# Attention of one core: VectorE combines a unit between the next one's two minima, ScalarE copies transposed probabilities between two exponentials

## The reference, cut to what matters

```python
# 4 heads, 1024 tokens, causal; q and k have two components of 64 each, v has 128
a[c] = softmax(q[:, c] @ k[:, c].T + causal_mask)          # c = 0, 1
attn = rms_norm((a[0] - lam * a[1]) @ v) * subln_w * (1 - lambda_init)
# recurrence, per group of 128 channels (4 groups)
r, i = sigmoid(xc @ w_gate_a + b_a), sigmoid(xc @ w_gate_x + b_x)   # xc: 4-tap causal conv
h[t] = exp(-8 * softplus(lru) * r) * h[t-1] + sqrt(1 - decay**2) * i * xc
y = h * gelu(gr)
```

## Time and profile before

| | us |
|---|---|
| median of 3 runs | 4649.63 (4648.69 to 4650.72) |
| profiled execution | 4649.02 |
| its span | 4647.2 |
| TensorE busy | 4526.9 (97% of the span) |
| VectorE busy | 2670.9 (57%) |
| ScalarE busy | 1728.5 (37%) |
| attention stage | about 3547 to 3743 of the span |

### The profile page before, as it was taken

How to read it: one execution, slowest core, us unless ns; L and a number is a source line. 1 busy time by engine, 2 the same in 40 slices (tenths; PEclk the granted TensorE clock), 3 DMA queues, 4 the chain that set the end, 5 groups by cost and what they waited for, 6 DMA issues and landing times. The chain is left out here.

```text
span 4647.2 us, 66517 instructions
## 1 busy us (share of the span) xinstructions
PE 4526.9 (97%) x27608; PEld 3674.0 (79%) x27608; DVE 2670.9 (57%) x3938; ACT 1728.5 (37%) x2924; POOL 457.6 (10%) x371
## 2 busy tenths in 40 slices
PE   7999999999999999999999799899999989999999
PEld 4888877778999999999999444688777567888887
DVE  3245545555637777777777686546453755555543
ACT  3234443444424544555444333211343742111111
POOL 0000000000002333332335000000010000000000
PEclk8999999999999999999999999999999999999999
DMA  5244344434430110111021352423210021122222
GB/s 210 99 145 150 131 147 141 145 132 150 168 120 15 46 54 33 62 43 59 28 100 47 98 179 86 150 104 118 82 46 19 19 113 64 68 77 73 100 87 95
DMA packets 155978, 441.79 MB, mean 95 GB/s; under 512 B 17168, under 2 KB 47120, under 8 KB 140448
## 3 DMA queue, kind: packets, MB, share of 16 engines
q1 hardware_dynamic: 140624, 383.98, 23.8%
q0 software_dynamic: 9296, 32.58, 2.0%
q10 hardware_dynamic: 5760, 20.97, 1.2%
HBM read 294.86 MB, written 141.56 MB: 94 GB/s over the span
## 5 line engine op out<-in xcount | busy, mean ns | idle before, releaser
L202 PE MATMUL pr_ps<-uhl,w_split 128*128 128x512 f32 (+1 forms) x1520 | 586.1, 386 | 3.1 <-DVE w_split L145 2.2
L206 PE MATMUL pr_ps<-uhl,w_split 128*128 128x512 f32 (+1 forms) x1520 | 571.1, 376 | 0.0
L205 PE MATMUL pr_ps<-uhl,w_split 128*128 128x512 f32 (+1 forms) x1520 | 570.6, 375 | 0.0
L1583 DVE TENSOR_TENSOR b_G<-b_ps,cst 128x512 fp32r<-128x512 f32 x560 | 381.4, 686 | 65.1 <-PE b_ps L1362 61.7
L138 ACT ACTIVATE w_split<-share 128x2048 fp32r<-128x2048 f32 x64 | 122.6, 1915 | 700.8 <-DVE ou_vc L3304 271.1
L202 PEld LDWEIGHTS pr_ps<-uhl,w_split 128*128 128x128 f32 x1520 | 286.7, 189 | 81.5 <-issue 29.2
L205 PEld LDWEIGHTS pr_ps<-uhl,w_split 128*128 128x128 f32 x1520 | 286.9, 189 | 56.1 <-issue 5.8
L206 PEld LDWEIGHTS pr_ps<-uhl,w_split 128*128 128x128 f32 x1520 | 286.6, 189 | 52.6
L1124 POOL TENSOR_SCALAR b_Mr<-b_tri 128x512 fp32r<-128x512 f32 x80 | 117.7, 1489 | 1878.4 <-DVE b_tri L1567 1878.4
L202 PE MATMUL ou_ps<-ou_a,w_split 128*128 128x512 f32 x704 | 277.1, 394 | 7.7 <-DVE ou_a L2160 7.7
L205 PE MATMUL ou_ps<-ou_a,w_split 128*128 128x512 f32 x704 | 275.4, 391 | 0.0
(11 more groups left out here) (498 smaller groups left out, 10082.3 us busy)
## 6 DMA issues: line engine op xcount, KB each, us to landing
w_ring<-in_w_in SPq DMA_DIRECT2D x41, 1024.0 KB, 5.5
proj<-pr_stage SPq DMA_DIRECT2D x160, 256.0 KB, 2.0
share<-in_w_up SPq DMA_DIRECT2D x24, 1024.0 KB, 4.8
ar<-share SPq DMA_DIRECT2D x32, 512.0 KB, 2.8
b_AR<-ar SPq DMA_DIRECT2D x64, 256.0 KB, 2.9
pr_raw<-proj SPq DMA_DIRECT2D x48, 256.5 KB, 3.5
ada<-in_ada_w SPq DMA_DIRECT2D x24, 512.0 KB, 5.6
ff<-ou_vc ACTq DMA_DIRECT2D x24, 512.0 KB, 2.6
```

The source lines that it names most:

```text
L202: mm = nc.tensor.matmul(dst, a[0], b[0], start=start, stop=False)
L205: nc.tensor.matmul(dst, a[0], b[1], start=False, stop=False)
L206: return nc.tensor.matmul(dst, a[1], b[0], start=False, stop=stop)
L1583: L[x]["dve"].done(V.tensor_tensor(Gs[x][m % 2][:], heads(x, 0 if m else 1), rep(K(f"lev{m}"), 4), ALU.mult), f"{n}.G{m}")
```

## The change

TensorE's `sc` takes one component: its order becomes sc(n, 0), tr(n-2), sc(n, 1), then gates or flip, then av(n-3), one unit later than before. ScalarE: exp(n, 0), turn_out(n-2), take(n-3), exp(n, 1), then the work of t. VectorE: peak(n, 0), soft(n-1), peak(n, 1), then the work of t. The sums are kept for a whole head (`sm` grows to two heads of eight units), so that the reciprocal of component 0 is taken once per head in `mean`, `soft` takes that of component 1 alone and its copy to `r0` goes. Work moves between units: square from 1 to 3, mean from 2 to 4, norm from 4 to 5, scale from 5 to 6, run from 7 to 0 of the next head (head 3's stays at 7), leave from 0 to 1, the taps from 4 to 7 to 1 to 4. ScalarE gets two explicit loads of function tables, the set with Ln and Exp behind `rise`, and that with Exp and Tanh ahead of `open_a` in heads 1 to 3; the Ln on a dummy before the end goes.

```diff
--- before.py
+++ after.py
@@ -2587,7 +2587,7 @@
         sem = lambda m: nc.alloc_semaphore(f"at_{m}")
         sb = lambda n, s, d=F32: ctx.enter_context(nc.sbuf_tensor("at_" + n, s, d))
         p, aT = sb("p", [P, 2, 2, T]), sb("aT", [P, 2, T // P, P])
-        nb, sm, rc = sb("nb", [P, 2, 2]), sb("sm", [P, 2, 2]), sb("rc", [P, 2, 2])
+        nb, sm, rc = sb("nb", [P, 2, 2]), sb("sm", [P, 2, 8, 2]), sb("rc", [P, 2])
         ratio = sb("ratio", [P, 2])
         r0 = sb("r0", [P, 2, 8])
         lp, lam = sb("lp", [P, 2]), sb("lam", [P, 4])
@@ -2615,7 +2615,6 @@
         y_stored, head_stored = ([sem(f"{n}{b}") for b in range(2)] for n in ("y_stored", "stored"))
         S = ps[:, 0:4].rearrange("p (c b) f -> p c (b f)", c=2)
         TR = ps[:, 4:6].rearrange("p a f -> p (a f)")
-        warm = ctx.enter_context(nc.sbuf_tensor("at_warm", [P, 1], F32))
         flat_at = lambda h, x: ps[:, 4 + x] if h + 1 == A_HEADS else ps[:, 1 + 2 * x]
         with nc.Block() as block:
             @block.sync
@@ -2643,19 +2642,18 @@
                 nc.tensor.matmul(ps[:, 7, 0:2], K("heads64"), lp[:], start=True, stop=True).then_inc(lam_s, 1)
                 pe.wait_ge(rounded, 2)
 
-                def sc(n):
+                def sc(n, c):
                     h, t = units[n]
                     w = (t + 1) * P
-                    if t == 4:
+                    if t == 4 and c == 0:
                         pe.wait_ge(th_x, h + 1)
-                    for c in range(2):
-                        if n >= 1:
-                            pe.wait_ge(exp_ready, 2 * n - 1 + c)
-                        r = slice(64 * c, 64 * c + 64)
-                        for b in range(0, w, HALF):
-                            nc.tensor.matmul(S[:, c, b:min(w, b + HALF)], qk[r, h, t * P:(t + 1) * P],
-                                             qk[r, 4 + h, b:min(w, b + HALF)], start=True, stop=b + HALF < w)
-                        nc.tensor.matmul(S[:, c, t * P:w], id_r[:], mask_r[:], start=False, stop=True).then_inc(scores, 1)
+                    if n >= 1:
+                        pe.wait_ge(exp_ready, 2 * n - 1 + c)
+                    r = slice(64 * c, 64 * c + 64)
+                    for b in range(0, w, HALF):
+                        nc.tensor.matmul(S[:, c, b:min(w, b + HALF)], qk[r, h, t * P:(t + 1) * P],
+                                         qk[r, 4 + h, b:min(w, b + HALF)], start=True, stop=b + HALF < w)
+                    nc.tensor.matmul(S[:, c, t * P:w], id_r[:], mask_r[:], start=False, stop=True).then_inc(scores, 1)
 
                 def tr(n):
                     h, t = units[n]
@@ -2699,7 +2697,10 @@
                     mm.then_inc(flipped, 1)
                 for n in range(NU):
                     h, t = units[n]
-                    sc(n)
+                    sc(n, 0)
+                    if n >= 2:
+                        tr(n - 2)
+                    sc(n, 1)
                     if t == 1:
                         gates(h, 0)
                     if t == 2:
@@ -2707,10 +2708,10 @@
                     if t == 0 and h >= 2:
                         pe.wait_ge(exp_ready, 2 * n)
                         flip(h - 2)
-                    if n >= 1:
-                        tr(n - 1)
-                    if n >= 2:
-                        av(n - 2)
+                    if n >= 3:
+                        av(n - 3)
+                tr(NU - 2)
+                av(NU - 3)
                 tr(NU - 1)
                 av(NU - 2)
                 pe.wait_ge(exp_ready, 2 * NU)
@@ -2730,12 +2731,15 @@
                 act.wait_ge(hb_ready, 2)
 
                 def exp(n, c):
-                    w = (units[n][1] + 1) * P
+                    h, t = units[n]
+                    w = (t + 1) * P
                     act.wait_ge(nb_ready, 2 * n + c + 1)
+                    if h >= 2 and t == 0 and c == 0:
+                        act.wait_ge(meaned, h - 1)
                     if n >= 2 and c == 0:
                         act.wait_ge(turned, n - 1)
                     A(p[:, n % 2, c, 0:w], S[:, c, 0:w], ACT.Exp, scale=-1.0, bias=nb[:, n % 2, c:c + 1],
-                      accum_out=sm[:, n % 2, c:c + 1]).then_inc(exp_ready, 1)
+                      accum_out=sm[:, h % 2, t, c:c + 1]).then_inc(exp_ready, 1)
 
                 def turn_out(n):
                     w = (units[n][1] + 1) * P
@@ -2806,29 +2810,33 @@
                 for n in range(NU):
                     h, t = units[n]
                     exp(n, 0)
+                    if n >= 2:
+                        turn_out(n - 2)
+                    if n >= 3:
+                        take(n - 3)
                     exp(n, 1)
-                    if n >= 1:
-                        turn_out(n - 1)
-                    if n >= 2:
-                        take(n - 2)
                     if t == 0 and h >= 2:
                         end(h - 2)
                     if t == 1:
+                        if h:
+                            nc.scalar.preload_act_table_set("exp_and_others")
                         open_a(h)
-                        if h:
-                            square(h - 1)
                     if t == 2:
                         open_x(h)
                         decay(h)
                     if t == 3:
                         decay2(h)
                         bend(h)
-                    if t == 4 and h:
-                        norm(h - 1)
+                        if h:
+                            square(h - 1)
                     if t == 5:
                         rise(h)
-                A(warm[:], G["eps"][:, 0:1], ACT.Ln)
+                        nc.scalar.preload_act_table_set("natural_log_exp_and_others")
+                        if h:
+                            norm(h - 1)
+                turn_out(NU - 2)
                 turn_out(NU - 1)
+                take(NU - 3)
                 take(NU - 2)
                 take(NU - 1)
                 square(A_HEADS - 1)
@@ -2879,12 +2887,9 @@
                     w = (t + 1) * P
                     b = n % 2
                     dve.wait_ge(exp_ready, 2 * n + 2)
-                    s.done(V.reciprocal(rc[:, b], sm[:, b]))
+                    s.done(V.reciprocal(rc[:, b:b + 1], sm[:, h % 2, t, 1:2]))
                     s.wait()
-                    if t == 0 and h >= 2:
-                        dve.wait_ge(meaned, h - 1)
-                    s.done(V.tensor_copy(r0[:, h % 2, t:t + 1], rc[:, b, 0:1]))
-                    s.done(V.scalar_tensor_tensor(ratio[:, b:b + 1], sm[:, b, 0:1], lam[:, 3:4], rc[:, b, 1:2], ALU.mult, ALU.mult))
+                    s.done(V.scalar_tensor_tensor(ratio[:, b:b + 1], sm[:, h % 2, t, 0:1], lam[:, 3:4], rc[:, b:b + 1], ALU.mult, ALU.mult))
                     s.wait()
                     V.scalar_tensor_tensor(p[:, b, 0, 0:w], p[:, b, 1, 0:w], ratio[:, b:b + 1], p[:, b, 0, 0:w],
                                            ALU.mult, ALU.add).then_inc(diff, 1)
@@ -2892,6 +2897,7 @@
                 def mean(h):
                     dve.wait_ge(squared, h + 1)
                     s.done(V.tensor_reduce(ms[:], sq[:], AX.X, ALU.add))
+                    s.done(V.reciprocal(r0[:, h % 2], sm[:, h % 2, :, 0]))
                     s.wait()
                     s.done(V.tensor_tensor(ms[:], ms[:], r0[:, h % 2], ALU.mult))
                     s.wait()
@@ -2942,29 +2948,31 @@
                     V.tensor_tensor(y[:, k % 2], xc[k % 2][:], gr[:, k], ALU.mult).then_inc(y_ready, 1)
                 for n in range(NU):
                     h, t = units[n]
+                    peak(n, 0)
                     if n >= 1:
                         soft(n - 1)
-                    peak(n, 0)
                     peak(n, 1)
                     if n == 0:
                         for j in range(4):
                             tap(0, j)
-                    if t == 2 and h:
-                        mean(h - 1)
+                    if t == 0 and h:
+                        run(h - 1)
+                    if t == 1 and h:
+                        leave(h - 1)
+                    if 1 <= t <= 4 and h + 1 < RT:
+                        tap(h + 1, t - 1)
                     if t == 3:
                         admit(h)
                     if t == 4:
                         spare(h)
-                    if t == 5 and h:
-                        scale(h - 1)
+                        if h:
+                            mean(h - 1)
                     if t == 6:
                         enter(h)
-                    if t == 7:
+                        if h:
+                            scale(h - 1)
+                    if t == 7 and h + 1 == A_HEADS:
                         run(h)
-                    if t == 0 and h:
-                        leave(h - 1)
-                    if t >= 4 and h + 1 < RT:
-                        tap(h + 1, t - 4)
                 soft(NU - 1)
                 leave(RT - 1)
                 mean(A_HEADS - 1)
```

## The result

The changed kernel takes 4696.82 us (median of 4 runs, 4696.14 to 4709.35), against 4650.18 of the kernel before beside it: a ratio of 1.0106, 95% interval 1.0089 to 1.0124. It is slower by 47 us where I had forecast no change, and lies outside my range (4636 to 4664).

What follows compares the result with a forecast made beforehand. TensorE was taken as tightest, VectorE and ScalarE not far. Head 0 -0.3, three head stretches at 44.65, 45.6 and 44.0 and tail -2.0 gave -1.6 us; one slow stretch of 1.7 made about 0: 4650 us, range 4636 to 4664.

Steps and rivals of the forecast that it cites:

- The stop before the widest transposes: TensorE's wait of 2.04 us (2.93 at the first head) before unit 7's eight transposes, behind VectorE's scan: would go.
- ScalarE's wait behind take(n-3): take(n-3) waits for TensorE's last product of iteration n, exp(n,1) and side work queue behind; costly in units 0 to 2.
- My hand-carried stops: TensorE stops from carrying four queues through a middle head: 6.85 us in a stretch of 45.6.
- The ones of units 5 to 7: TensorE stops before the scores of units 5, 6 and 7, waiting for ScalarE: 1.4, 0.95 and 2.0 us.
- Head 0 to its unit 7: Start of the attention stage: unit 7 would start at 3583.2 against 3583.47, -0.3 us.
- Table loads in the stage: ScalarE's function-table loads in attention: 14 instead of 19, one being 1.28 us.
- From the last take to the end of the tail: Chain behind the last take: 9.66 us to the second copy's end, less a 1.28 load, plus a small reciprocal.
- The whole tail: Attention's end: 24.3 us instead of 26.26, -2.0; bounds 24.3 and +1.7 for the clock of flip and av.
- the slow stretch: TensorE at lower clock after stops, put back into the sum: one stretch of 1.7 us; bounds 0 and +27.
- A clock under 0.9: Sign of being wrong: granted clock under 0.9 in the three head stretches would mean the clock decided.
- short stops: TensorE stops: 0.65 us drew no slow stretch before, 2.0 to 2.9 did; most new ones, 1.0 to 1.4, judged nearer the short.
- My rival of the clock: Units 2 to 7 of heads 1 to 3: more stops lower TensorE's clock, nine stretches give 15 us, 4665; chance 0.12.

Runs made afterwards that it cites:

- a later run: Kernel before with four superfluous table loads (two sets in turn) on ScalarE ahead of exp(n,0) of unit 1 in heads 1 to 3: 4663.86 us.
- 64-row filler: Changed kernel plus a 64-row, 384-column product ahead of each half of scores from unit 3: 4665.88 us; with two table loads ahead of unit 3's exp(n,0) too, 4720.67.
- 128-row filler with a stop: Changed kernel plus a 128-row, 384-column product ahead of each half of scores from unit 3, and two table loads ahead of unit 3's exp(n,0) in heads 1 to 3: 4670.61 us.
- The change with av beside tr: Changed kernel with TensorE's av(n-3) moved right behind tr(n-2), ahead of the second half of scores: 4666.14 us.
- the dual: Kernel before with av(n-2) between the halves of scores: 4654.96 us; with one table load ahead of unit 4's exp(n,0) in heads 1 to 3 too, 4680.71.

## Why the prediction was wrong

**Right, step by step.** The stop before the widest transposes went. ScalarE's wait behind take(n-3) was there. My hand-carried stops: before the second gate product 1.3 (measured 1.08), before unit 4 of a later head 1.0 (0.84). The ones of units 5 to 7 in later heads can't be read: at half clock TensorE is late itself. Head 0 to its unit 7: -0.3 forecast, +0.2 measured. Table loads in the stage fell from 19 to 14. From the last take to the end of the tail the prediction's terms give 8.45 (9.66 less 1.28, and the small reciprocal); measured from the take to the end of the last copy, 8.5:

```profile
3783.92 0.28 ACT L2756 ACTIVATE at_raw<-at_ps 128x128 f32<-128x128 f32 x1 [2.38 <-PE at_ps L2675]
...
3791.74 0.68 ACT L2775 ACTIVATE share<-at_ps,at_sub_w 128x512 f32<-128x512 f32 x1
```

The whole tail took 29.2 us where 24.3 was forecast: the last low stretch reaches into it up to 3778. The Trainium skill's drain behind a table load (ScalarE: Activation LUTs, What ACT_TABLE_LOAD costs) did not appear here either: 1.29 us from the load at 3665.72 to open_a.

**The step that failed** is the one in the sum that puts "the slow stretch" back. I priced a fall of the clock at 1.7 us, the value of the stretches in the trace of before, allowed 0 to 27 us for all of them and took 1.7. Three long stretches of 37.5 to 41 us cost 14 to 16 us a head: the head stretches came out at 58.7, 60.7 and 60.6 us for my 44.65, 45.6 and 44.0, at a granted clock of 0.67 to 0.68. A clock under 0.9 was one of the signs of being wrong that I had set. Two assumptions were in it. First, that short stops (0.65 us drew none, 2.0 and more did) are the safe side: 0.84 and 1.40 us were followed by a fall here, and 0.43 us in a later run. Second, that the length of a low stretch belongs to the chip and not to the work: in the kernel before, each head's fall came at unit 0 (one is in the earlier trace rows), at wide 128-row products, and was repaired at once. I saw that the stops moved from there to units 3 to 7 and named that place, but not that the work there has 64 rows. My rival of the clock had the right cause and sign, but it counted nine short stretches of 1.7 us, not three long ones; I gave it 0.12 and 4665 us, a third of what the clock cost.

The loss thus needs the stops of the new order (by take behind av, and by the side work) and their place in the units where 64-row scores are most of the work; the split of the 128-row work adds to it. Take any away and most of the loss is gone: the stops (64-row filler, 4666), the rows (128-row filler with a stop, 4671), the split (4666, where two stops of a head also gave way to one of 1.52 us). The first two are shown; how much of the third is the split itself is not.

**Open.** Why a stop of 1.5 us in the old order is followed by 7 us in one head and 27 in the next, why one of 0.7 in head 0 is followed by 10 us in one kernel and 31 in another that does the same up to there, and why 0.43 us sometimes is enough, no run tells. Each kernel's stretches are read from one execution, and how much they vary between executions no trace here shows. The change with av beside tr has fewer stops than the change besides its order, so what the split is worth in its 31 us is only estimated, by the dual: 15 to 18 us for three stops. That a long low stretch ends in the narrow units, with their wide av and gates, is seen in the traces of the change and of the 64-row filler, but no run tried those apart.

## What to carry to other kernels

In this case a fall of TensorE's clock was priced by what the engine computed after it, not by the stop: before moving a wait, look whether the products behind it have few rows, and keep it ahead of dense full-height products. Where an engine near its bound feeds TensorE in such a part, a moved step that adds a stop of 1 us can cost 15. Change one part at a time: the scan's move alone was worth 13 us, and was hidden under a loss of 60.

## What the runs showed of the hardware

The granted clock stayed at its lower level for up to 51.0 us (64-row filler) in which the profile has TensorE busy without a break. The Trainium skill (TensorE: Matmul & The Clock Gate, Part 1) says that the clock follows how busy the engine has been, and that a sustained busy stretch brings it up. By that rule the low stretches here would have been short; the three of 37.5 to 41 us in the change, and the 51.0, contradict it where 64-row products are most of the work, and the measurement decides. Equal columns with 64 instead of 128 rows made 50 us of difference with a stop ahead of them, and none (4666 and 4665) without one. Stops of 1.25 and 1.08 us in the old order drew no low stretch in two heads, and one of 0.43 us in the same order drew one of 17.1.
